# The gated recurrence's keys and running sums made during the in-projection, and the experts' bias rows laid out in parts

## The reference

```python
proj = jnp.dot(h, w_in[l]) + b_in[l]
aq, ak, av, hq, hf, hi, hg = jnp.split(proj, split_at, axis=-1)
attn = sliding_window_attention(aq, ak, av, attn_sinks[l])
# recurrence
q = jax.nn.silu(q)
f = lb + (1.0 - lb) * jax.nn.sigmoid(f_logit)      # forget values
logf = jnp.log(f)
k = 1.0 - f                                        # keys
bc = jnp.cumsum(chunks(logf), axis=3)              # running sums
att = jnp.einsum('bhtk,bhtsk,bhsk->bhts', q_, jnp.exp(rel), k_)
# expert block
hid = jnp.dot(xblk, w1[e]) + b1[e]
glu = jnp.minimum(hid[:, 0::2], SWIGLU_LIMIT)
lin = jnp.clip(hid[:, 1::2], -SWIGLU_LIMIT, SWIGLU_LIMIT)
return jnp.dot(act, w2[e]) + b2[e]
```

## Time and profile before

| What | us |
|---|---|
| Median of 3 runs (lowest, highest) | 2268.34 (2266.12, 2269.85) |
| The profiled execution, its own time | 2264.41 |
| Its span in the profile | 2262.8 |
| In-projection, PE full | about 55 to 290.5 |
| Attention | 290.5 to 396.3 |
| Forget values, keys, logarithms, sums | 396.3 to 411.6 |
| Recurrence | 411.6 to about 560 |
| Expert jobs, PE full | 722 to 2236 |
| PE, PEld, DVE, ACT busy over the span | 92%, 79%, 71%, 59% |

### The profile page before, as it was taken

How to read it: one execution, slowest core, us unless ns; L and a number is a source line. 1 busy time by engine, 2 the same in 40 slices (tenths; PEclk the granted TensorE clock), 3 DMA queues, 4 the chain that set the end, 5 groups by cost and what they waited for, 6 DMA issues and landing times. The chain is left out here.

```text
span 2262.8 us, 40586 instructions
## 1 busy us (share of the span) xinstructions
PE 2079.4 (92%) x11750; PEld 1781.1 (79%) x11751; DVE 1605.1 (71%) x2242; ACT 1333.0 (59%) x1884; POOL 380.8 (17%) x446
## 2 busy tenths in 40 slices
PE   6999978577994999999999999999999999999993
PEld 5888857566873979788897888978897888979883
DVE  5121166997555878778787787878788787877875
ACT  5211234454343766767667676677667676675865
POOL 2000000000124111213112131122111131121311
PEclk9999989899995999999999999999999999999997
DMA  5211110001336988879798797989798897988978
GB/s 173 59 40 55 47 56 1 7 14 60 133 100 201 313 256 291 300 246 334 256 322 292 256 333 255 327 285 350 255 334 280 275 330 243 334 277 278 328 241 297
DMA packets 259028, 499.82 MB, mean 221 GB/s; under 512 B 34273, under 2 KB 35298, under 8 KB 258808
## 3 DMA queue, kind: packets, MB, share of 16 engines
q1 hardware_dynamic: 241850, 455.95, 58.9%
q0 software_dynamic: 17120, 43.13, 8.0%
q10 hardware_dynamic: 4, 0.02, 0.0%
HBM read 461.90 MB, written 37.13 MB: 221 GB/s over the span
## 5 line engine op out<-in xcount | busy, mean ns | idle before, releaser
L1746 DVE TENSOR_TENSOR wlo<-raw,whi 128x1024 fp32r<-128x1024 f32 x774 | 930.3, 1219 | 81.6 <-ACT whi L1244 52.8
L1244 ACT ACTIVATE whi<-raw 128x1024 fp32r<-128x1024 f32 x775 | 846.8, 1117 | 208.0 <-PE ps L948 139.8
L946 PE MATMUL ps<-xT,whi 128*128 128x320 f32 x1920 | 522.0, 348 | 0.0
L948 PE MATMUL ps<-xT,wlo 128*128 128x160 f32 x1920 | 454.5, 237 | 0.0
L948 PEld LDWEIGHTS ps<-xT,wlo 128*128 128x128 f32 x1920 | 367.7, 191 | 0.6
L946 PEld LDWEIGHTS ps<-xT,whi 128*128 128x128 f32 x1920 | 361.7, 188 | 2.1
L1992 POOL DMA_INDIRECT acc_d<-y,icur x64 | 103.3, 1613 | 961.1 <-ACT y L1278 940.3
L586 PE MATMUL ps<-whi,xT 128*128 128x512 f32 x544 | 218.8, 402 | 0.0
L586 PE MATMUL ps<-whi,aT 128*128 128x512 f32 x512 | 212.9, 416 | 4.2 <-DVE aTl L1805 3.8
L588 PE MATMUL ps<-whi,xT 128*128 128x512 f32 x544 | 213.9, 393 | 0.0
L587 PE MATMUL ps<-wlo,xT 128*128 128x512 f32 x544 | 213.7, 393 | 0.0
(11 more groups left out here) (291 smaller groups left out, 3577.1 us busy)
## 6 DMA issues: line engine op xcount, KB each, us to landing
raw<-in_w SPq DMA_DIRECT2D x776, 512.0 KB, 6.6
raw<-in_w_in SPq DMA_DIRECT2D x16, 512.0 KB, 3.6
xs<-in_x SPq DMA_DIRECT2D x8, 512.0 KB, 7.8
raw<-in_w_out SPq DMA_DIRECT2D x8, 512.0 KB, 3.7
mix<-in_x SPq DMA_DIRECT2D x8, 512.0 KB, 4.2
acc_d<-mix SPq DMA_DIRECT2D x8, 512.0 KB, 5.2
h_d<-h SPq DMA_DIRECT2D x8, 512.0 KB, 2.8
mix<-acc_d SPq DMA_DIRECT2D x8, 512.0 KB, 8.0
```

The source lines that it names most:

```text
L946: pe.matmul(o2, wh[:, a, cols], xT2[:, :, k, 0:JOB_T], start=q == 0 and a == 0, stop=False, skip_group_check=True)
L948: m = pe.matmul(o, wl[:, a, cols], xT2[:, 0, k, 0:JOB_T], start=False, stop=q == QUARTERS - 1 and a == 1, skip_group_check=True)
L1244: act.activation(parted(slot(whis, s)), paired(slot(raws, s), s), ACT.Copy).then_inc(split_hi, 1)
L1746: dve.tensor_tensor(parted(slot(wlos, s)), paired(slot(raws, s), s), parted(slot(whis, s).bitcast(F32)), ALU.subtract).then_inc(split_lo, 1)
```

## The change

Four things change.

- **Moved in time.** Forget values and keys are made on DVE right after unit 1 of the in-projection, the logarithms on ACT at the same place, the running sums on DVE after unit 2. `reset` moves to a place that is free then, and POOL fills it earlier.
- **Keys through DRAM.** The keys are written to a tile `keys` that later becomes `hv`, sent to a new DRAM tensor `keys_d` and brought back into the recurrence half of the tile `mix` after the in-projection. Diagonal and products read them there, through `key_cols(hd)`: eight pieces of 128 values with a step of 1024, where `hk` was one run of 1024.
- **Start of attention.** PE makes `scores(0)` after chain 1 of unit 5 is taken and `scores(1)` after chain 3. DVE makes the alibi table in two halves, the first after chain 3 of unit 5, and `add_bias(0)` after chain 5.
- **Bias rows parted.** Each 512 values of the `w1` bias are sorted into gate and linear halves once, when `bph` and `bpl` are made (three instructions on each of ACT and POOL where there was one). The matmuls L990 and L951 then read them in one run.

The core of the diff:

```diff
-    hk = at("hk", A + 32 * KB, [P, HH, T])
-    reset = at("reset", A + 52 * KB, [P, T])
+    keys = at("keys", B + 32 * KB, [P, NT, 512])
+    reset = at("reset", B + 68.5 * KB, [P, T])
+        def key_cols(hd):
+            return mix[:, :, ATTN_W + hd * P:ATTN_W + (hd + 1) * P]
+        def by_parts(b):
+            return b[0:NE, 0:2 * FF].rearrange("p (c two n) -> p c two n", c=4, two=2)
+        def by_pairs(b):
+            return b[0:NE, 0:2 * FF].rearrange("p (c n two) -> p c two n", c=4, two=2)
 PE
-            pe.wait_ge(*taken(5, 7))
+            pe.wait_ge(*taken(5, 1))
             scores(0)
+            pe.wait_ge(*taken(5, 3))
             scores(1)
+            pe.wait_ge(*taken(5, 7))
-                    pe.wait_ge(keys_set, HH)
+                    pe.wait_ge(keys_in, 16)
-                                  hk[:, hd, t * P:(t + 1) * P], hq[:, hd, t * P:(t + 1) * P],
+                                  key_cols(hd)[:, t, :], hq[:, hd, t * P:(t + 1) * P],
-                            pe.matmul(o, brow[:, c * UNIT + 256 * i + odd:c * UNIT + 256 * (i + 1):2], ones2[:, 0:JOB_T],
+                            pe.matmul(o, brow[:, c * UNIT + 256 * odd + P * i:c * UNIT + 256 * odd + P * (i + 1)], ones2[:, 0:JOB_T],
-                        if q == 0 and c < 4:
-                            pe.matmul(o.rearrange("p (two n) -> p two n", two=2), ones2[:, 0:P],
-                                      brow[:, bias:bias + UNIT].rearrange("p (n two) -> p two n", two=2),
-                                      start=True, stop=False)
-                        elif q == 0:
+                        if q == 0:
                             pe.matmul(o, (ones2, ones1)[b][:, 0:n], brow[:, bias:bias + UNIT], start=True, stop=False)
 ACT
-            act.activation(bph[:, :], bp[:, :], ACT.Copy).then_inc(bias_hi, 1)
+            act.activation(by_parts(bph), by_pairs(bp), ACT.Copy)
+            act.activation(bph[NE:NE + 1, 0:2 * FF], bp[NE:NE + 1, 0:2 * FF], ACT.Copy)
+            act.activation(bph[:, 2 * FF:BW], bp[:, 2 * FF:BW], ACT.Copy).then_inc(bias_hi, 1)
+                if n == 1:
+                    for hd in range(HH):
+                        act.wait_ge(keys_set, hd + 1)
+                        act.activation(hf[:, hd, :], hf[:, hd, :], ACT.Ln).then_inc(logs_set, 1)
 DVE
+                        if c == 3:
+                            dve.wait_ge(quarter_used, 4 * 6)
+                            alibi_set(0)
+                        elif c == 5:
+                            add_bias(0)
+                if n == 1:
+                    dve.wait_ge(bias_out, 32)
+                    for hd in range(HH):
+                        link(dve.tensor_scalar(hf[:, hd, :], hf[:, hd, :], oml[:, hd:hd + 1], lb[:, hd:hd + 1],
+                                               ALU.mult, ALU.add))
+                        dve.tensor_scalar(keys[:, :, hd * P:(hd + 1) * P], hf[:, hd, :].rearrange("p (t n) -> p t n", n=P),
+                                          -1.0, 1.0, ALU.mult, ALU.add).then_inc(keys_set, 1)
+                elif n == 2:
+                    dve.wait_ge(reset_set, 1)
+                    for hd in range(HH):
+                        dve.wait_ge(logs_set, hd + 1)
+                        dve.tensor_tensor_scan(hf[:, hd, :], reset[:, :], hf[:, hd, :], 0.0, ALU.mult,
+                                               ALU.add).then_inc(sums_set, 1)
+            alibi_set(1)
             add_bias(1)
+            dve.wait_ge(keys_in, 16)
-                                  for z in (hp[:, s % 2, :], hk[:, hd, :], he[:, s % 2, :]))
+                                  for z in (by_tile(hp[:, s % 2, :]), key_cols(hd), by_tile(he[:, s % 2, :])))
 POOL
-            pool.tensor_tensor(bpl[:, :], bp[:, :], bph[:, :].bitcast(F32), ALU.subtract).then_inc(bias_lo, 1)
+            link(pool.tensor_tensor(by_parts(bpl), by_pairs(bp), by_parts(bph).bitcast(F32), ALU.subtract))
+            pool.wait_ge(keys_set, HH)
+            pool.dma_start(keys_d, keys[:, :, :]).then_inc(keys_out, 16)
             for c in range(8):
                 pool.wait_ge(*taken(5, c))
                 pool.dma_start(hg_d[c * P:(c + 1) * P, :], hgs[:, c % 2, :]).then_inc(hg_out[c % 2], 16)
+            pool.wait_ge(keys_out, 16)
+            pool.dma_start(mix[:, :, ATTN_W:D], keys_d).then_inc(keys_in, 16)
```

More of the change, by code:

```diff
@@ L1137, in _ @@
                 square(t, 0, attT[1][:, 0:4, :].rearrange("p a b -> p (a b)"))
-            for hd in range(HH):
-                act.wait_ge(keys_set, hd + 1)
-                act.activation(hf[:, hd, :], hf[:, hd, :], ACT.Ln).then_inc(logs_set, 1)
             def outs(hd):
@@ L1409, in _, with alibi_set, add_bias @@
                                           ALU.subtract).then_inc(turned_lo, 1)
+            def alibi_set(kv):
+                for h in range(GROUP * kv, GROUP * kv + GROUP):
+                    link(dve.scalar_tensor_tensor(out=alibi[:, h, :], in0=dist[:, :], scalar=-SLOPES[h],
+                                                  in1=closed[:, :], op0=ALU.mult, op1=ALU.add))
+            def add_bias(b):
+                n, kv = divmod(b, 2)
+                dve.wait_ge(scored, b + 1)
+                if b >= 2:
+                    dve.wait_ge(probs_turned, 2 * b - 2)
+                lo = P if n == 0 else 0
+                s = score[:, kv, :, lo:]
+                link(dve.tensor_tensor(s, ps[:, 2 * kv:2 * kv + 2, :].rearrange("p a (i k) -> p (a i) k", i=2)[:, :, lo:],
+                                       alibi[:, GROUP * kv:GROUP * kv + GROUP, lo:], ALU.add))
+                dve.sem_inc(score_added, 1)
+                link(dve.tensor_reduce(stat[:, 0, b, :], s, AX, ALU.max))
+                link(dve.tensor_tensor(stat[:, 0, b, :], stat[:, 0, b, :], sinks[:, GROUP * kv:GROUP * kv + GROUP], ALU.max))
+                dve.tensor_scalar(stat[:, 1, b, :], stat[:, 0, b, :], -1.0, None, ALU.mult)
+                link(dve.tensor_tensor(stat[:, 2, b, :], sinks[:, GROUP * kv:GROUP * kv + GROUP], stat[:, 0, b, :], ALU.subtract))
+                dve.sem_inc(maxed, 1)
             for n in range(6):
@@ L1916, in _ @@
             pool.wait_ge(bias_hi, 1)
[L1917 to L1925 removed]
+            link(pool.tensor_tensor(by_parts(bpl), by_pairs(bp), by_parts(bph).bitcast(F32), ALU.subtract))
+            link(pool.tensor_tensor(bpl[NE:NE + 1, 0:2 * FF], bp[NE:NE + 1, 0:2 * FF],
+                                    bph[NE:NE + 1, 0:2 * FF].bitcast(F32), ALU.subtract))
+            pool.tensor_tensor(bpl[:, 2 * FF:BW], bp[:, 2 * FF:BW], bph[:, 2 * FF:BW].bitcast(F32),
+                               ALU.subtract).then_inc(bias_lo, 1)
+            pool.wait_ge(tinit_out, 16)
             link(pool.memset(reset[:, :], 1.0))
@@ L1929, in _ @@
             pool.wait_ge(keys_set, HH)
+            pool.dma_start(keys_d, keys[:, :, :]).then_inc(keys_out, 16)
+            for c in range(8):
+                pool.wait_ge(*taken(5, c))
+                pool.dma_start(hg_d[c * P:(c + 1) * P, :], hgs[:, c % 2, :]).then_inc(hg_out[c % 2], 16)
+            pool.wait_ge(quarter_used, 4 * 6)
+            pool.wait_ge(keys_out, 16)
+            pool.dma_start(mix[:, :, ATTN_W:D], keys_d).then_inc(keys_in, 16)
+            pool.wait_ge(heads_out, 2 * NT)
+            iota(iotaE[:, :], [[1, NE]], 0)
+            iota(tok[:, :], [[P, NT]], 1)
             pool.wait_ge(rec_out, 2 * HH)
```

54 lines of the change are left out of this document (14 added, 40 removed).

## The result

| | before | after | forecast |
|---|---|---|---|
| Median, us | 2268.77 | 2247.57 | 2231 |
| Lowest to highest | 2266.12 to 2269.85 | 2242.59 to 2248.91 | 2219 to 2243 |
| Profiled execution | 2264.41 | 2242.59 | 2227.5 |
| Ratio of the times | | 0.9908, 95% interval 0.9891 to 0.9925 | 0.984 |

The change makes the kernel 0.9% faster. The direction was right and the size was not: 21 us arrived of 37, and the median lies above the range. The profile of the changed kernel answers the old rows one by one. First the busy time by stage, in the columns of the earlier trace rows: projection, the joint between attention and recurrence, the jobs.

What follows compares the result with a forecast made beforehand. PE was taken to bound in-projection and expert jobs, DVE the stretch between attention and recurrence. 15.6 + 2.4 + 5.3 + 13.6 = 36.9 us off the profiled 2264.4 gave 2227.5, or 2231 against the median; range 2219 to 2243.

Steps and rivals of the forecast that it cites:

- the sentence on the narrow bias rows: Narrow expert jobs: PE bounds and splits lead by six slots, so faster w1 bias matmuls save the whole 15.6 us.
- the one on transfers: Narrow jobs: transfers bound them, PE only waits for weights and 15.6 us are lost: 2247; chance 0.05.
- Bias rows, as PE time: Narrow jobs' w1 bias: spacing falls from 0.69 to 0.46 us, 68 times 0.23, 15.6 us.
- The rival of the free step: Narrow w1 bias: the step of two costs nothing, only the front gains 18.9 us: 2249; chance 0.06.
- Wide bias rows: Wide jobs' bias rows as weights: 0.01 us saved each, 240 times, 2.4 us.
- 12 was excluded: Wide jobs, rival: weight loads are the whole difference, 0.05 us each, 12 instead of 2.4: 2222; chance 0.14.
- Start of the attention: First exponential of the attention starts at 299.8 instead of 305.15; 5.3 us earlier, carried through 16 blocks unchanged.
- The cover: Attention start: block 0 is ready before ACT needs it, by a thin margin; if late, up to 5.3 us slip.
- The rival of the clock: Attention start: `hgs` rounds or a falling PE clock eat the earlier start, 5.3 us lost: 2236; chance 0.08.
- Joint: Between attention and recurrence: values, keys and sums leave DVE's way, first product comes earlier, gain 13.6 us.
- Hidden work, keys, products: Moved DVE and ACT work hides in the in-projection, key transfers and eight-piece products cost nothing; all priced at 0.
- POOL's rows: POOL's low part of the bias rows grows from 6.80 to 11.3 us in three instructions, hidden, priced at 0.

Runs made afterwards that it cites:

- a_x21: Changed kernel with the activation's last turn at slot 19 instead of 20 and the turns of x at 18 to 21: 2227.06 us, ratio 0.9805 to before.
- a_fill: Changed kernel plus 48 matmuls without use on PE at the end of the recurrence: 2244.78 us, ratio 0.9889 to before.
- a_relief: Changed kernel with DVE making low parts for only half the rows in slots 8 to 23 of narrow jobs: 2243.91 us, ratio 0.9885 to before.
- a_turn19: Changed kernel with the activation's last turn at slot 19 instead of 20 and the second turn of x at 20: 2236.16 us, ratio 0.9846 to before.

## Why the prediction was wrong, by its own steps

- **The step that failed** is the sentence on the narrow bias rows: "PE is what bounds there, and the splits run ahead of it by six slots, so nothing else is late in its place." PE is busy 37.78 of 37.90 us in a narrow job, but the transfers are at a share of 0.97 beside it, and the lead is 4.9 slots in the mean, where the last turn needs five. What is late in PE's place is the weights' transfers, which hold up the splits, and with them `aTl`: 14.2 us of waiting for 4.2, and 1.9 with the transfers halved. Of 15.6 + 2.4 us the profile kept 6.4 in the jobs, the rows alone 7 in the median. The full share of the earlier trace rows, 1498.90 of 1514.00, was read as room on the others, from a row that averages two kinds of job.
- **The rival that came true** was the one on transfers, which had 0.05: "if 0.92 us less for PE in each of 17 jobs only makes PE wait for weights, 15.6 us are lost: 2247". The median is 2247.57. That the two numbers meet is partly luck: by the profile 11.6 us and not 15.6 were lost to the waits, and another 4.4 to the clock. What I held against it, the lead of six slots and the wide jobs between, was not looked up, though the wide jobs do give something back once the turns allow it (a_x21): a count of finished splits at PE's slot starts would have shown 4.9. What it did not have is the form: the wait is put down to `aTl` on DVE, and only relief of either side shows whose it is.
- **Bias rows, as PE time: right.** 0.47 for 0.69 us, and 19.3 us in the jobs once both reliefs are in. The rival of the free step fell with it; the Trainium skill's rule on cache lines ("Advanced Engine Details and Errata", SBUF Cachelines) does not hold for this reading.
- **Wide bias rows: right in size.** 533.7 to 531.4 us for the `w1` parts of 15 wide jobs, 2.3 for the forecast 2.4; 12 was excluded.
- **Start of the attention: right**, 299.76 for 299.8. The cover held. The shift of 5.4 us shrank to 2.1 within the attention, behind 23.9 us at half clock, and was 6.1 at the end of the heads (396.3 and 390.2). The rival of the clock was thus at work, and was paid back, which no step of the forecast had; what gave it back was not followed up.
- **Joint: right.** 19.6 - 6.1 = 13.5 us for the forecast 13.6; both together 19.6 for 18.9.
- **A term that was missing**: the stretch from the first product to the jobs, which kept 4.4 us less in the profile and 2.2 in the mean of fifteen profiles. The clock is its likely cause: a_fill, which holds the clock up there, got the time back at the start of its jobs.
- **Hidden work, keys, products: right**, all at nothing. POOL's rows took 4.64 + 4.60 + 3.26 = 12.5 us for the estimated 11.3.

In the profile: 36.9 + 0.7 (front) - 4.4 (clock) - 11.6 (rows) = 21.6, for 21.8 measured.

## What to carry to other kernels

Where a loop runs jobs of two kinds, read each kind's window by itself before saying what bounds it: a mean of 0.88 was 0.97 and 0.83. With a resource at 0.97 beside the bound, as here, time taken from the bound may not be won. Relieve that resource and the engine that the wait names one after the other: here the wait named DVE, and only the transfers' relief removed it. Then look at which queued step uses up the lead first: three entries in the tables of turns were worth 20 us on top of the change's 21.

## What the runs showed of the hardware

- A moving operand of 4-byte values with a step of two costs a 512-column matmul 0.23 us (median from its start to the start of the second matmul behind it, 68 times: 0.69 us with the step, 0.46 without), and the same step in a 128-column weight load about 0.01 (240 times: 0.119 us to the next matmul, 0.111 without).
- A matmul of 128 columns with `ident`, whole float32 values, takes 0.234 us at a granted clock of 1.00, 5.62 / 24, and stands as two rows in the profile. One on a high or low part is one row and takes half of that, 0.11 us.
- Idle work kept the granted clock at 1.00 at the end of the recurrence, yet no kernel with it could be shown faster than its neighbour without, and two were slower (2232.19 and 2236.66 for 2226.88 and 2227.06).
- Where the granted clock falls differs between executions of the same front: with the first product at 395.5 us in both, the jobs start at 703.60 us in a_relief (3.4 us at half clock at the end of the recurrence) and at 709.35 in a_turn19 (17).
- Products of DVE that read their second operand in eight pieces took 685 ns, no more than in one piece (686).
